# Feed-forward norm of a hybrid encoder layer: squares by column halves, scaling on two engines, a weight's remainder behind it, and the last tile's transposes at the end

## What is computed

```
x = x + merged @ w_out[l]
h = rmsnorm(x, norm_ffn[l])            # y = x * rsqrt(mean(x*x) + 1e-6), then * w
gu = h @ ffn_w_gate_up[l]              # 1024 x 5632
x = x + (silu(gu[..., :2816]) * gu[..., 2816:]) @ ffn_w_down[l]
return rmsnorm(x, final_norm)
```

## Time and profile before

| | |
|---|---|
| timed, three runs | 1082.17 us median (1081.99, 1082.17, 1085.79) |
| the profiled execution: its time | 1086.66 us |
| its span | 1084.9 us |
| mean granted clock of TensorE | 0.988 |
| TensorE busy | 1044.1 us, 96% |
| VectorE busy | 522.3 us, 48% |
| ScalarE busy | 380.0 us, 35% |
| GpSimd busy | 134.8 us, 12% |
| read from memory | 83.64 MB, 80 GB/s over the span |

### The profile page before, as it was taken

The page is one execution under the profiler, slowest core; times in us unless marked ns, Lnnn a source line. Parts: engine busy times, 40 slices in busy tenths (PEclk is TensorE's granted clock), DMA queues, the critical chain, the costliest instruction groups (busy, mean ns, idle before and its releaser), DMA issues.

```text
span 1084.9 us, 14413 instructions
## 1 busy us (share of the span) xinstructions
PE 1044.1 (96%) x5926; PEld 868.4 (80%) x5926; DVE 522.3 (48%) x731; ACT 380.0 (35%) x570; POOL 134.8 (12%) x207
## 2 busy tenths in 40 slices
PE   8999999999989998999999999989999999999995
PEld 6889798856668887878888888878888888888884
DVE  6775447477766778354351515452323232322313
ACT  6536546654422211432332322342323232311312
POOL 4000001536752241000000000000000000000201
PEclk9999999999999998999999999999999999999998
DMA  9332320000100013104242316414242424232201
GB/s 297 121 88 78 117 69 2 1 3 9 21 11 1 2 40 117 59 25 131 65 129 78 117 63 229 117 39 117 78 117 78 116 78 117 78 117 102 94 19 77
DMA packets 104000, 87.18 MB, mean 80 GB/s; under 512 B 13109, under 2 KB 93697, under 8 KB 103936
## 3 DMA queue, kind: packets, MB, share of 16 engines
q1 hardware_dynamic: 102288, 81.80, 24.9%
q0 software_dynamic: 1488, 4.40, 1.1%
q10 hardware_dynamic: 160, 0.07, 0.0%
HBM read 83.64 MB, written 2.62 MB: 80 GB/s over the span
## 4 chain that ended last, share of the span: by engine, by line
PE 88%; DVE 6%; issue 2%; ACT 2%; POOL 1%; DMA 1%; SPq 0%; DVEq 0%; POOLq 0%; ACTq 0%
PE psum L900 24%; PE psum L901 23%; PE psum L902 23%; PE psum L1205 2%; PE psum L1212 1%; PE psum L1225 1%; PE psum L1348 1%; PE psum L1277 1%; PE psum L1179 1%; PE psum L1304 1%; PE psum L1334 1%; PE psum L1360 1%; PE psum L1099 1%; PE psum L1028 1%; POOL Zs L803 1%
## 5 line engine op out<-in xcount | busy, mean ns | idle before, releaser
L900 PE MATMUL psum<-hT_hi,w_hi 128*128 128x512 f32 (+1 forms) x712 | 279.8, 393 | 4.4 <-DVE w_lo L1974 2.7
L902 PE MATMUL psum<-hT_hi,w_lo 128*128 128x512 f32 (+1 forms) x712 | 278.1, 391 | 0.0
L901 PE MATMUL psum<-hT_lo,w_hi 128*128 128x512 f32 (+1 forms) x712 | 278.0, 391 | 0.0
L1974 DVE TENSOR_TENSOR w_lo<-w_raw,w_hi 128x2048 fp32r<-128x2048 f32 (+2 forms) x81 | 167.5, 2068 | 227.7 <-ACT w_hi L1517 227.7
L1517 ACT ACTIVATE w_hi<-w_raw 128x2048 fp32r<-128x2048 f32 (+2 forms) x82 | 141.4, 1725 | 160.8 <-PE psum L902 148.6
L900 PEld LDWEIGHTS psum<-hT_hi,w_hi 128*128 128x128 f32 (+1 forms) x712 | 134.2, 188 | 34.2 <-DVE w_lo L1974 3.6
L902 PEld LDWEIGHTS psum<-hT_hi,w_lo 128*128 128x128 f32 (+1 forms) x712 | 133.8, 188 | 28.8
L901 PEld LDWEIGHTS psum<-hT_lo,w_hi 128*128 128x128 f32 (+1 forms) x712 | 134.1, 188 | 27.8
L1974 DVE TENSOR_TENSOR psum<-gate_act,psum 128x512 f32<-128x512 f32 x22 | 15.3, 696 | 119.6 <-PE psum L902 119.6
L900 PE MATMUL psum<-w_hi,act_hi 128*128 128x512 f32 x176 | 68.5, 389 | 0.0
L901 PE MATMUL psum<-w_lo,act_hi 128*128 128x512 f32 x176 | 68.5, 389 | 0.0
(11 more groups left out here) (311 smaller groups left out, 1574.4 us busy)
## 6 DMA issues: line engine op xcount, KB each, us to landing
w_raw<-in_w_in_dram SPq DMA_DIRECT2D x23, 1024.0 KB
w_raw<-in_ffn_w_gate_up_dram SPq DMA_DIRECT2D x44, 512.0 KB
w_raw<-in_ffn_w_down_dram SPq DMA_DIRECT2D x10, 1024.0 KB
w_raw<-in_mem_w_kv_dram SPq DMA_DIRECT2D x4, 1024.0 KB
w_raw<-in_w_out_dram SPq DMA_DIRECT2D x4, 1024.0 KB
x_tok<-in_x_dram SPq DMA_DIRECT2D x4, 512.0 KB, 5.3
w_raw<-in_w_branch_mla_dram SPq DMA_DIRECT2D x4, 512.0 KB
w_raw<-in_w_branch_dn_dram SPq DMA_DIRECT2D x4, 512.0 KB
```

What stands on the lines that cost most here:

```text
L900: pe.matmul(o, s_hi, m_hi, start=first, stop=False)
L901: pe.matmul(o, s_hi, m_lo, start=False, stop=False)
L902: return pe.matmul(o, s_lo, m_hi, start=False, stop=last)
L1974: return dve.tensor_tensor(o, a, b, op)
```

## The change

- The squares are summed over 512 columns at a time. The left halves of all four tiles are squared on ScalarE right behind their residuals, ahead of the conversion of `("wo", 1, 1)`; the right halves as each becomes whole. The mean's instruction adds the two sums and epsilon.
- Tiles 0 and 1 are scaled on ScalarE, tile 2 on VectorE, tile 3 half on each. Three new semaphores carry this: `rstd_ffn`, `xs_by_act`, `xs_by_dve`.
- VectorE puts the next residual between a tile's mean and its root.
- VectorE's `prep` of `("gu", 0)` moves from ahead of the right residuals to behind the eight splits. ScalarE's conversion of that block stays where it was.
- TensorE turns tiles 0 to 2 in k = 0 to 3, then the same tiles in k = 4 to 7, then tile 3 in all eight.
- Later counts of the squares' semaphore are moved by four.

```
--- before.py
+++ after.py
@@ -526,6 +526,9 @@
         glu_ready = sem("glu_ready")
         glu_hi = sem("glu_hi")
         x2_ready = sem("x2_ready")
+        rstd_ffn = sem("rstd_ffn")
+        xs_by_act = sem("xs_by_act")
+        xs_by_dve = sem("xs_by_dve")
         y_ready = [sem(f"y_ready{t}") for t in range(NT)]
         xw_ready = sem("xw_ready")
         rstd_final = sem("rstd_final")
@@ -1473,13 +1476,20 @@
                     m.then_inc(full(("h2T", k)), 1)
 
 
-            for t in range(NT):
-                pe.wait_ge(xs_ready, 2 * NT + NM + t + 1)
+            scaled_by = ((xs_by_act, 1), (xs_by_act, 2), (xs_by_dve, 1))
+            for t in range(NT - 1):
+                pe.wait_ge(*scaled_by[t])
                 for k in range(KD // 2):
                     turn_x1(k, t)
             for k in range(KD // 2, KD):
-                for t in range(NT):
+                for t in range(NT - 1):
                     turn_x1(k, t)
+            pe.wait_ge(xs_by_dve, 2)
+            for k in range(KD // 2):
+                turn_x1(k, NT - 1)
+            pe.wait_ge(xs_by_act, 3)
+            for k in range(KD // 2, KD):
+                turn_x1(k, NT - 1)
             for f in range(NF):
                 need(("gu", f))
                 by_feature(("g", f), ("gu", f), 0, hT_hi, hT_lo, source="h2T" if f == 0 else None)
@@ -1916,14 +1926,34 @@
                 for j in range(2):
                     act.wait_ge(merge_sum, 2 * c + j + 1)
                     A(mT_hi[:, 2 * c + j, :], part[:, j, :]).then_inc(merge_hi, 1)
+            def ffn_squares(half, t):
+                released(act, ("wo", half, t))
+                squares(x1[:, t, 512 * half:512 * half + 512], square3[:, 512 * half:512 * half + 512],
+                        small[:, 0, NT * half + t:NT * half + t + 1], D ** -0.5)
+
+            def ffn_root(t):
+                root("ffn", small[:, 2, t:t + 1], small[:, 1, t:t + 1], t)
+
+            def ffn_scale(t, cols):
+                act.wait_ge(rstd_ffn, t + 1)
+                A(xs1[:, t, cols], x1[:, t, cols], scale=rstd[:, t:t + 1]).then_inc(xs_by_act, 1)
+
             for half in range(2):
                 for kk in range(2):
                     prep(after(("wo", half, kk)))
+                if half == 0:
+                    for t in range(NT):
+                        ffn_squares(0, t)
             root_tables()
-            for t in range(NT):
-                released(act, ("wo", 1, t))
-                squares(x1[:, t, :], square3[:, :], small[:, 0, t:t + 1])
-                root("ffn", small[:, 2, t:t + 1], small[:, 1, t:t + 1], t)
+            ffn_squares(1, 0)
+            ffn_root(0)
+            for t in range(2):
+                ffn_squares(1, t + 1)
+                ffn_scale(t, slice(0, D))
+                ffn_root(t + 1)
+            ffn_squares(1, 3)
+            ffn_root(3)
+            ffn_scale(3, slice(512, D))
             for k in range(KD):
                 split_T(("h2T", k), hT_hi[:, k, :], V_FFN + k)
             for f in range(NF):
@@ -2545,20 +2575,33 @@
                 ins.then_inc(free(key), 1)
 
             for half in range(2):
-                for kk in range(2):
+                for kk in range(2 - half):
                     prep(after(("wo", half, kk)))
                 if half == 0:
                     dve.wait_ge(x1_landed, 16)
                 for t in range(NT if half == 0 else 1):
                     residual(half, t)
+
+            def ffn_mean(t):
+                dve.wait_ge(ssq_ready, 2 * NT + NM + t + 1)
+                dve.scalar_tensor_tensor(out=small[:, 1, t:t + 1], in0=small[:, 0, t:t + 1], scalar=EPS,
+                                         in1=small[:, 0, NT + t:NT + t + 1], op0=ALU.add, op1=ALU.add).then_inc(ms_ready, 1)
+
+            def ffn_scale(t, cols):
+                dve.wait_ge(rstd_ffn, t + 1)
+                dve.tensor_scalar(xs1[:, t, cols], x1[:, t, cols], rstd[:, t:t + 1], None, ALU.mult).then_inc(xs_by_dve, 1)
+
             for t in range(NT):
+                ffn_mean(t)
                 if t + 1 < NT:
                     residual(1, t + 1)
-                dve.wait_ge(ssq_ready, NT + NM + t + 1)
-                rsqrt("ffn", slice(t, t + 1), D, rstd[:, t:t + 1], t)
-                dve.tensor_scalar(xs1[:, t, :], x1[:, t, :], rstd[:, t:t + 1], None, ALU.mult).then_inc(xs_ready, 1)
+                if t == NT - 1:
+                    ffn_scale(NT - 2, slice(0, D))
+                root_of("ffn", slice(t, t + 1), rstd[:, t:t + 1], t, rstd_ffn)
+            ffn_scale(NT - 1, slice(0, 512))
             for k in range(KD):
                 split_T(2 * KD + 4 + k, ("h2T", k), hT_hi[:, k, :], hT_lo[:, k, :], V_FFN + k)
+            prep(after(("wo", 1, 1)))
             for f in range(NF):
                 prep(after(("gu", f)))
                 key = ("u", f)
@@ -2582,7 +2625,7 @@
                 for t in range(NT if half == 0 else 1):
                     add_glu(half, t)
             def final_means(b):
-                dve.wait_ge(ssq_ready, 3 * NT + NM + 2 * b + 2)
+                dve.wait_ge(ssq_ready, 4 * NT + NM + 2 * b + 2)
                 dve.scalar_tensor_tensor(out=small[:, 1, 2 * b:2 * b + 2], in0=small[:, 0, 2 * b:2 * b + 2], scalar=EPS,
                                          in1=small[:, 0, NT + 2 * b:NT + 2 * b + 2], op0=ALU.add, op1=ALU.add).then_inc(ms_ready, 1)
```

## The result

The changed kernel took 1091.04 us in the median of five runs (1089.48 to 1093.74), before in the same comparison 1082.18 us (1081.99 to 1085.92): a ratio of 1.0068, 95% interval 1.0052 to 1.0084. It is slower: by 7.4 us if the ratio is applied to before's 1082 us, by 8.9 us between the two medians. Forecast were 6.4 us and 1088.6 us. So the time lies in the stated range (1085.0 to 1092.5), 2.4 us above the point, and outside the narrower range that the forecast gave itself (1087 to 1090). Where one of them is held against the changed kernel, which was timed beside another set of runs of before, two ratios are subtracted.

What follows compares the result with a forecast made beforehand. TensorE was taken to bound the kernel, holding 88% of the chain that ended last. 4.2 us of waiting plus 2.2 us of clock gave +6.4 us on 1082.17, so 1088.6 us, range 1085.0 to 1092.5.

Steps and rivals of the forecast that it cites:

- The mark in before: Feed-forward norm's end: at full pace throughout, before's first gate product would start at 714.82 us; later means a later end.
- The last tile: Feed-forward norm: tile 2 scaled at 708.3 us, last tile's first transpose at 710.35 instead of 710.76 us, 0.4 us gained.
- Splits and remainder: VectorE before the first gate product: eight splits end at 716.8 us, the weight remainder adds 2.21 us, restart at 719.0 us.
- Without the clock: First gate product: restart at 719.0 us against the mark of 714.82 us, 4.2 us later.
- The clock at the restart: First gate products after TensorE's 7.6 us idle: slow clock costs 2.2 us, between 1.7 and 3.1.
- The sum: Whole kernel: 4.2 us of waiting plus 2.2 us of clock make +6.4 us, between 5.9 and 7.3.
- A clock that costs nothing more: Rival, chance 0.14: at the restart the clock costs no more than before, leaving +4.2 us, 1086.4 us.
- Slow transposes: Rival, chance 0.08: 16 transposes ahead of the splits run at 0.193 us each, adding 1.0 us: +7.4 us, 1089.6 us.
- A remainder that is not waited for: Rival, chance 0.05: first gate product starts at 712.2 us without waiting for the weight remainder, 2.6 us gained, 1079.6 us.
- Late loads: Rival, chance 0.03: fourth gate/up weight lands after 738 + 6 us, TensorE waits; 10 us or more, 1092 and above.
- The cover ahead: ScalarE's conversion of the last output-projection weight slips about 1.5 us, with 5 us of cover, costing nothing.
- The signs: Expected profile: gate product waits 7 to 8 us for the remainder, clock 0.5 for 3 to 6 us, last transposes near 711.4.

Runs made afterwards that it cites:

- e10: The kernel before, unchanged, one further execution: 1081.92 us.
- e2: The kernel before with only the remainder of the first gate/up weight moved behind the eight splits: 1092.01 us, ratio 1.0078 to before.
- e1: The changed kernel with the remainder of the first gate/up weight back ahead of the right residuals: 1083.62 us, ratio 0.9984 to before.
- e6: e1 with the transposes back in the old order, tile 3's first four right behind tile 2's: 1081.08 us, ratio 0.9968 to before.
- e3: The changed kernel with the weight remainder between VectorE's last scaling and its eight splits: 1083.20 us, ratio 0.9980 to before.
- e8: The changed kernel with the weight remainder made twice in the same place: one execution of 1091.99 us.
- e4: The changed kernel with 28 unused products on TensorE between the first split and the first gate product: 1089.46 us, ratio 1.0044 to before.

## Why the prediction was right, and where its terms were off

The mechanism is the forecast one: TensorE waits for the remainder, the splits ahead of it lie bare, and the restart comes at the lower clock. Part of the agreement of the figure is luck, as the first and the sixth point show.

- **The mark in before, and what it was added to.** I put it at 714.82 us, 9.3 us behind the start of the last product; measured 9.2 us. But this is the value of an execution that loses its clock in the norm: its 20 transposes took 3.86 us, at full clock they take 2.40 us (e10, e2). One of four executions of before keeps the clock and has 7.6 us, and it took 1081.92 us. I took the difference from an execution of 1086.66 us and added it to a median of 1082.17 us. Of the clock's price in before I counted only the 0.2 us at the first product, and left out the 1.5 us of the transposes. Against an execution near 1082 us the stage is 15.0 - 7.6 = 7.4 us longer, against one like the profiled one 5.8 us; my 6.4 us lie between.
- **The last tile.** Forecast: the third tile scaled 2.8 us behind the start of the last product (708.3), measured 705.39 - 702.58 = 2.8 us. The 0.4 us that I gave to the five other parts was too little: e2 and the changed kernel differ in exactly these parts, and the restart is 14.0 - 13.25 = 0.7 us earlier. The 16 transposes ahead of the last tile's take 0.118 us each and not 0.129; the rest of the difference lies between the transposes and the first split. With the remainder ahead of the residuals the five parts take the stage from 7.6 us (e10, full clock) to 6.6 or 6.4 us (e1, e6), 0.9 to 1.1 us, and they spare TensorE the second rest, behind which before mostly loses 1.6 us more.
- **Splits and remainder.** Forecast restart 719.0 us, 13.5 us behind the last product; measured 13.25 us in three executions. That TensorE waits for exactly this instruction is shown by e2, e3 and e8.
- **Without the clock** I had 4.2 us; e4's stage of 13.4 us, whose clock is kept, less 9.2 us is the same 4.2 us. But the 9.2 us hold before's own loss of clock. With the clock kept in both it is 13.4 - 7.6 = 5.8 us.
- **The clock at the restart.** Forecast 2.2 us, between 1.7 and 3.1. Stage less restart is 1.7, 2.0 and 1.6 us, but some 0.1 to 0.2 us of this stand also where the clock is kept (e1, e4, e10), and e4 makes it 1.4 to 1.9 us. So the term was too high by about half a microsecond and its range began too high; e2, with 3.0 us and a slow stretch of 5.9 us, is the one near its upper end. The place to which I kept nearest was less firm than it looked: the rest of 2.33 us at 484 us kept its clock in 11 of the 14 profiles, in all three of the changed kernel among them. The Trainium skill (TensorE: Matmul & The Clock Gate, Part 1) says that the count of slow products changes from run to run; the stages of 14.8 to 15.3 us agree. The two recoveries of one trace that the prediction names lie behind different rests and could not show it.
- **The sum.** Three changed profiles have 15.0 us in the mean, four of before (3 x 9.2 + 7.6) / 4 = 8.8 us: 6.2 us. That this is so near to 6.4 us is luck in part: a restart 0.25 us too late and a clock term about 0.5 us too high stood against a mark that holds before's own loss of clock. The times give 7.4 us, with an interval of 5.6 to 9.1 us. The 1.2 us between lie inside it; what of them is the uneven loss of clock ahead of the stage stays open.
- **The rivals.** A clock that costs nothing more: refuted by the 0.43 us products of the changed kernel and by e4. Slow transposes: not seen, 24 took 2.84 us in each changed profile. A remainder that is not waited for: not so, but its figure, 2.6 us gained, is what e1's stage shows against 9.2 us, once the remainder is made ahead. Late loads: not so, the fourth and fifth weights were in by 724.4 us, and the fourth was taken at 740.74 us.
- **The cover ahead.** ScalarE's conversion of the last projection weight began 20.0 us ahead of the last product instead of 21.3 us. It slipped by 1.3 us, 1.5 were reckoned, and nobody waited.
- **The signs.** The wait of 7 to 8 us for the remainder is there (7.60 us), and so is the lower clock for 3 to 6 us at the restart (3.3 us). The last transposes end 5.65 us behind the start of the last product, 5.9 were forecast.

## What to carry to other kernels

Seven of the eight splits that feed TensorE block by block cost nothing in before, since TensorE multiplied while they were made. With one instruction that the first product needs put behind them, the whole splitting stood bare. So ask for each moved instruction what its reader waits for next, not how long it takes: against the place ahead of the residuals, the same 2.3 us cost 0.6 us ahead of the splits and 8.4 us behind them. And take a clock's price from several executions, since a rest of TensorE that costs the clock in one does not in another; and add a difference only to a time of the kind of execution that it was read from.

## What the runs showed of the hardware

Two rests of 1.96 and 1.40 us with four transposes between cost the clock in three of four executions of one program and not in the fourth, with the same rests to 0.01 us; e2, with the same rests, kept it too. A rest of 2.33 to 2.36 us cost it in 3 of 14 profiles, the one of 7.6 us in all three of the changed kernel, and there the clock fell while TensorE stood still. With such losses, at the norm and at the waits ahead of it, go the times of before from 1081 to 1088.5 us. How much each place costs is measured for the norm alone (1.6 us); for the others it is argued from where the executions come to the stage. Transposes run at the full clock: 20 in 2.40 us and 24 in 2.84 us, against 3.76 to 4.53 us for 20 where the lower clock came in between.
